# Two tiles of the normed activations in the second feed-forward part: beside the others from the second group on

## What is computed

```python
def conv_gated_mlp(h, w_up, conv_w, conv_b, w_down):
    gate, up = jnp.split(h @ w_up, 2, axis=-1)
    return (jax.nn.gelu(dwconv_centred(gate, conv_w, conv_b), approximate=True) * up) @ w_down
...
    x = x + g2 * conv_gated_mlp(modulate(rmsnorm(x, norm2_g[l]), sh2, sc2), *ffn)
...
    return rmsnorm(x, final_norm_g)
```

## Time and profile before

| | |
|---|---|
| median of 3 runs | 2564.16 us (2562.82 to 2564.85) |
| profiled execution | 2563.17 us, its span 2561.4 us |
| TensorE busy | 2536.9 us, 20794 matmuls |
| VectorE busy | 1927.4 us |
| ScalarE busy | 1138.3 us |
| granted clock of TensorE | 0.997 over the span |
| second feed-forward part | from 1825.5 us on |

### The profile page before, as it was taken

One profiled execution on the slowest core, in us unless ns is written; L12 is line 12 of the kernel. 1 busy time (PEld: TensorE's weight loads), 2 busy tenths in 40 slices (PEclk: granted clock), 3 DMA queues, 4 the chain that ended last, 5 costly groups with the idle time before them and its releaser, 6 DMA issues.

```text
span 2561.4 us, 49562 instructions
## 1 busy us (share of the span) xinstructions
PE 2536.9 (99%) x20794; PEld 2463.2 (96%) x20794; DVE 1927.4 (75%) x2458; ACT 1138.3 (44%) x1223; POOL 0.2 (0%) x4
## 2 busy tenths in 40 slices
PE   9999999999999999999999999999999999999998
PEld 9889999999999999999999899959999999999998
DVE  8978887897999888888893236777766666666667
ACT  6556554444544444444433234433444444444443
POOL 0000000000000000000000000000000000000000
PEclk9999999999999999999999999999999999999999
DMA  8766667767888888888773344424555555556553
GB/s 320 263 231 219 240 231 247 251 239 246 291 285 292 281 286 287 282 289 285 268 260 100 99 165 148 149 73 165 165 198 191 190 197 197 189 191 197 195 188 112
DMA packets 282890, 557.20 MB, mean 218 GB/s; under 512 B 10552, under 2 KB 16985, under 8 KB 282585
## 3 DMA queue, kind: packets, MB, share of 16 engines
q1 hardware_dynamic: 282568, 552.57, 64.3%
q10 hardware_dynamic: 144, 2.10, 0.2%
HBM read 552.53 MB, written 2.10 MB: 217 GB/s over the span
## 4 chain that ended last, share of the span: by engine, by line
PE 92%; DVE 6%; issue 1%; DMA 1%; ACT 0%; SPq 0%; DVEq 0%
PE PS L1826 80%; PE PS L1837 3%; PE PS L1840 3%; PE PS L1839 3%; DVE WL L1003 1%; PE PS L2073 1%; DVE ada1c L1269 0%; DMA RAW<-in_w_in 0%; DVE adac L1427 0%; PE PS L1904 0%; DVE SQ L1029 0%; PE PS L2176 0%; PE PS L2083 0%; PE PS L1893 0%; PE PS L2063 0%
## 5 line engine op out<-in xcount | busy, mean ns | idle before, releaser
L527 ACT ACTIVATE WH<-RAW 128x1024 fp32r<-128x1024 f32 x840 | 889.3, 1061 | 1278.9 <-PE PS L1826 1147.5
L1003 DVE TENSOR_TENSOR WL<-RAW,WH 128x1024 fp32r<-128x1024 f32 x840 | 1017.8, 1222 | 578.4 <-ACT WH L527 569.5
L1826 PE MATMUL PS<-XL,WH 128*128 128x256 f32 x4288 | 664.2, 277 | 0.0
L1826 PE MATMUL PS<-XH,WH 128*128 128x256 f32 x3752 | 586.0, 278 | 1.1 <-ACT WH L527 1.1
L1826 PEld LDWEIGHTS PS<-XL,WH 128*128 128x128 f32 x4288 | 569.1, 188 | 0.0
L1826 PE MATMUL PS<-XH,WL 128*128 128x256 f32 x3752 | 503.2, 277 | 0.0
L1826 PEld LDWEIGHTS PS<-XH,WH 128*128 128x128 f32 x3752 | 498.3, 188 | 3.5 <-DVE XL L1059 1.5
L1826 PEld LDWEIGHTS PS<-XH,WL 128*128 128x128 f32 x3752 | 461.5, 188 | 0.0
L1826 PE MATMUL PS<-HH,WH 128*128 128x256 f32 x1728 | 268.0, 277 | 1.2 <-DVE X L1388 1.2
L1826 PE MATMUL PS<-HL,WH 128*128 128x256 f32 x1728 | 266.2, 276 | 0.0
L1826 PE MATMUL PS<-HH,WL 128*128 128x256 f32 x1728 | 231.1, 276 | 0.0
(11 more groups left out here) (285 smaller groups left out, 1823.0 us busy)
## 6 DMA issues: line engine op xcount, KB each, us to landing
RAW<-in_w_ff SPq DMA_DIRECT2D x128, 1024.0 KB, 5.9
RAW<-in_w_in SPq DMA_DIRECT2D x111, 1024.0 KB, 5.1
RAW<-in_w_up SPq DMA_DIRECT2D x88, 1024.0 KB, 5.0
adab<-in_ada_w SPq DMA_DIRECT2D x128, 512.0 KB, 5.3
RAW<-in_w_down SPq DMA_DIRECT2D x44, 1024.0 KB, 5.0
ada1b<-in_ada_w SPq DMA_DIRECT2D x64, 512.0 KB, 6.0
RAW<-in_w_out SPq DMA_DIRECT2D x32, 1024.0 KB, 5.2
RAW<-in_w_oa SPq DMA_DIRECT2D x8, 1024.0 KB, 5.5
```

Of the source, the lines that this page charges most:

```text
L527: A(WH[:, c.base % 2, hs], RAW[:, c.base % SLOTS, hs], ACT.Copy).then_inc(hi_done, 1)
L1003: tt(WL[:, b, hs], RAW[:, c.base % SLOTS, hs], WH[:, b, hs].bitcast(f32), ALU.subtract)\
L1826: ins = MM(out[:, f, :], w[:, b, kk, f * P:(f + 1) * P], x, start=first and not low and n == 0 and f % 2 == 0, stop=last and low, skip_gro ...
```

## The change

A new buffer, `BEGIN_FIRST`, holds tiles 0 and 1 for the first group of the second feed-forward part alone. It lies at offset AR + 16 K + 96, which is 32 bytes past a multiple of 64, as XH_FIRST is. When ScalarE has written the last quarter of XH it writes tiles 0 and 1 a second time from the same NT and the same shift, now to their place in XH, and counts `first_again`. TensorE waits for that count ahead of the second group, and from then on reads all 16 tiles from XH. All stages before keep XH_FIRST. XL is not changed.

```diff
+        XH_FF2, XH_FF2_BEGIN = XH[:, :, :], XH[:, :, :]
...
+        BEGIN_FIRST = at("BEGIN_FIRST", [P, 2, T], AR + 16 * K + 96, f32r)
...
         def tile_of(x, k):
 
+            if k < 2 and x is XH_FF2_BEGIN:
+                return BEGIN_FIRST[:, k, :]
             return XH_FIRST[:, k, :] if k < 2 and x is XH else x[:, k, :]
...
                             for k in (2 * h, 2 * h + 1):
-                                ins = A(tile_of(XH, k), NT[:, k, :], ACT.Identity, bias=shift(k))
+                                ins = A(tile_of(XH_FF2_BEGIN if norm == N_FF2 else XH, k), NT[:, k, :],
+                                        ACT.Identity, bias=shift(k))
...
                 quarter_high(3)
+                if norm == N_FF2:
+                    for k in range(2):
+                        ins = A(XH_FF2[:, k, :], NT[:, k, :], ACT.Identity, bias=shift(k))
+                    ins.then_inc(sm["first_again"], 1)
...
+                        hi = XH_FF2_BEGIN if norm == N_FF2 else XH
                         for k in (2 * h, 2 * h + 1):
-                            ins = stt(tile_of(XL, k), NT[:, k, :], shift(k), tile_of(XH, k).bitcast(f32),
+                            ins = stt(tile_of(XL, k), NT[:, k, :], shift(k), tile_of(hi, k).bitcast(f32),
                                       ALU.add, ALU.subtract)
...
                 for s in range(SLOTS):
-                    wide(c.plus(s), q, s)
+                    wide(c.plus(s), q, s, xh=XH_FF2)
                 for s in range(SLOTS):
-                    wide(c.plus(4 + s), q.plus(1), s)
+                    wide(c.plus(4 + s), q.plus(1), s, xh=XH_FF2)
...
             for s in range(SLOTS):
-                wide(Place(C_FF2 + s), Place(Q_FF2), s, e=E_NORM4)
+                wide(Place(C_FF2 + s), Place(Q_FF2), s, e=E_NORM4, xh=XH_FF2_BEGIN)
+            pe.wait_ge(sm["first_again"], 1)
             for s in range(SLOTS):
-                wide(Place(C_FF2 + 4 + s), Place(Q_FF2 + 1), s)
+                wide(Place(C_FF2 + 4 + s), Place(Q_FF2 + 1), s, xh=XH_FF2)
```

More of the change, by code:

```diff
@@ L340, in build_program @@
             "pn_done tp_done pt_done pv2_done a2_done fu_ps fu_done fy_ps fq_done fy_ends fy_done mlp_ps mlp_arg mlp_sin hf_ps "
-            "hf_done fold_done ks_ps ks_done zt_ps zt_done zf_ps ys_done yi_ps hz_done mix_sq cw_done conv_a conv_b "
+            "hf_done fold_done ks_ps ks_done zt_ps zt_done zf_ps ys_done yi_ps hz_done mix_sq first_again cw_done conv_a conv_b "
             "conv_done gelu_done").split()
```

## The result

| us | before | after |
|---|---|---|
| median of 20 runs each | 2563.69 (2560.04 to 2566.32) | 2562.06 (2559.23 to 2591.92) |
| the 11 shorter runs of after | | median 2561.11 (2559.23 to 2562.60) |
| the 9 longer runs of after | | median 2588.84 (2584.81 to 2591.92) |
| profiled execution | 2563.17, span 2561.4 | 2588.84, span 2587.0 |

The ratio of the times, after to before, is **1.0038 (1.0020 to 1.0056)**. That is a mean over two kinds of runs: the changed kernel never took 2573 us, it took some 2561 us or some 2589. Its median of 2562.06 says little: had two of the runs gone the other way, it would be over 20 us higher. Eleven runs are 2.6 us faster than before, nine are 25.2 us slower than before. No run of before was longer than 2566.53 us, of 122 in all sessions.

What follows compares the result with a forecast made beforehand. TensorE, busy 2536.9 of 2561.4 us, was taken as the bound. 21 x 0.115 = 2.4 us off the 2564.16 us median, other terms zero, gave 2561.8 us; range: 2561.8 less some 2.8 us to 2564.2 plus 2.3 us.

Steps and rivals of the forecast that it cites:

- The gain: On TensorE, 21 gate and up groups no longer open with XH_FIRST, saving 0.115 us each, 2.4 us in all.
- The place as the cause: XH_FIRST's start 32 bytes past a multiple of 64 makes its group 0.11 to 0.12 us slower on TensorE.
- rival one: The tile's place is not what costs, so the change gains nothing: 2564.2 us; chance 0.09.
- ScalarE's two activations and the wait at no cost: Two activations (0.91 us) have over 6 us of cover; first_again is satisfied 7.3 us before the second group: zero cost.
- The slow pace and its price: A lasting TensorE pace, 117.7 against 113.3 ns, over 6144 matmuls of the remaining 128 chunks: 27.0 us lost.
- rival two: The wait for XL leaves TensorE slow and no XH_FIRST head ends it: 2588.8 us; chance 0.15.
- the word "reset": In before, 236 matmuls from 390.18 us were slow, 164 from 421.24 fast; the XH_FIRST head between seemed to reset the pace.
- the term for a lasting slow pace: TensorE's wait for XL at 1837.06 us should end fast as before, so 0 us was added to the sum.
- Nothing there sets the state off: Between 1850 and 2545 us only stretches with XH_FIRST are slow, so nothing there starts the slow pace.

Runs made afterwards that it cites:

- after_again: The changed kernel run again with nothing edited: 11 runs from 2559.58 to 2563.08 us, none long, ratio 0.9994.
- e_places: e_second with gate groups of steps 0 to 5 reading copies of tiles 0 and 1 at 0, 16, 32, 48, 8, 56 bytes past a multiple of 64: 2567.27 us.
- e_kicks_gate: e_second with 4 + j transposes between gate and up group of each step j, and displaced tiles at every step's gate group: 2578.46 us.
- e_thirteen: The changed kernel with 13 instead of 12 idle products ahead of the first group: 11 runs, 3 long (2587.51 to 2589.07 us), ratio 1.0014.
- e_second: The changed kernel with the second group also reading displaced tiles 0 and 1: medians 2561.13 and 2560.37 us in two sessions, 0 of 22 runs long.
- after_third: The changed kernel with nothing edited, on another chip: 12 runs, 9 from 2560.74 to 2563.00 us, 3 long (2586.16 to 2588.87), ratio 1.0012.
- e_swap: The changed kernel with VectorE making XL's third quarter ahead of NT's last: 12 runs, 5 long (2587.49 to 2591.66 us), ratio 1.0039.
- e_middle: The changed kernel with step 4's gate group reading displaced tiles: 12 runs, 9 from 2559.53 to 2563.29 us, others 2570.78, 2588.67, 2589.20; ratio 1.0014.
- e_middle_up: The changed kernel with step 4's up group reading displaced tiles: 11 runs, median 2561.43 us, none long, ratio 0.9993.
- e_kicks: e_second with 4 + j unread transposes at the start of each step j (0 to 9): 2579.11 us.
- e_eight_head: e_eight with step 4's up group opening with displaced tiles: 10 runs, median 2562.52 us, ratio 0.9997.
- e_eight: e_second with one break of 8 transposes at the start of step 4: 10 runs, median 2561.29 us, none long, ratio 0.9991.

## Why the prediction was partly right and missed

**The gain.** Its term was 21 x 0.115 = 2.4 us. In after_again, whose profile is one of 2561.80 us, the part from the first head to the last chunk is 2.37 us shorter than in before; the medians of the first session differ by 2.6 us (2563.69 to 2561.11). The price, the count and the claim that it all falls off TensorE were right, for an execution that stays fast.

**The place as the cause** (rival one the other way round). Right: e_places has no extra time at offset 0, and 0.08 and 0.15 us at 16 and 32.

**ScalarE's two activations and the wait at no cost.** Right: 0.90 us for the pair, ended at 1841.17, while TensorE came at 1849.22 without idle time.

**The slow pace and its price** (rival two). That the pace is a state that outlasts its cause, and its size, were right: 6144 x 4.4 = 27.0 us. The medians of the two kinds of runs of after are 27.7 us apart, and the profiles of after and after_again differ by 744.63 - 717.09 = 27.5 us; the rest is mostly the 92 or so matmuls between the gap and the second group, 0.4 us. The rival's 2588.8 us is the 2588.84 of the longer kind. The signs it was to be known by are all there: 0.47 us for four matmuls, 22.6 us for a group, 281 ns on HH.

**One reading under that rival was wrong.** The 236 matmuls from 390.18 to 417.96 us are not all on well-placed tiles, and the group that opens at 417.96 us is not the next one. A group opened with XH_FIRST at 395.36 us, was met slow and left TensorE slow (rows under e_kicks_gate). The heads near 56 and 463 us did the same. So the row on which the word "reset" rested held a head that reset nothing.

**The step that failed** is the term for a lasting slow pace, which the sum put at nothing, with the sentence that carried it: "the change puts nothing ahead of 1837.06 that moves a time, so the same wait should end the same way". The runs showed 27.7 us more in 9 of 20 runs, from a slow pace that in the profile starts at that wait, before either new activation and the wait for first_again. The chance of 0.15 went with the sentence. Two things were wrong with it.
- The outcome doesn't follow from the times that were compared at the wait. The gap in six profiles: how TensorE came to it, when it went on, how far that was after the eight matmuls ahead of it were over, and how it left:

| kernel | came | restart, us | late by, us | left |
|---|---|---|---|---|
| before | slow | 1837.06 | 0.09 | fast |
| after_again | slow | 1838.05 | 0.08 | fast |
| e_thirteen | slow | 1837.11 | 0.10 | **slow** |
| e_second | fast | 1838.39 | 0.30 | fast |
| after | fast | 1837.81 | 0.29 | **slow** |
| after_third | fast | 1835.15 | 0.30 | **slow** |

  (The lateness is the restart less the start of those eight and 8 x 117.7 or 113.3 ns.) In the other ten profiles that have the gap (all but e_swap) TensorE came fast, went on 0.30 or 0.31 us late and left fast. So of 13 that came fast two left slow, and of 3 that came slow one did: the same gap to 0.01 us, and either pace behind it. One execution of before was one throw, and I had read it as a rule. That the earlier trace rows show a wait that ended slow was in my hands, and I gave it the weight of an exception.
- The gap isn't the only place. TensorE already came to it slow in 3 of the 16 profiles, and e_swap, without the gap, had 5 long runs of 12. In before neither seems to matter, since 21 heads come after it: none of its 122 runs was long, while 18 of the 77 runs with this gap and without a head in the second group were long (after, after_again, after_third, e_middle, e_middle_up, e_thirteen; the run of 2570.78 us is counted). That a head in before ends a pace still slow at 1848 us is an inference; its one profile left the gap fast.

The consequence is the miss: the measured ratio, 1.0038 (1.0020 to 1.0056), lies on the side to which I had given 0.15, though the median lay in my range. I had also formed a range for one value, while the changed kernel has two. "Nothing there sets the state off" was right for the stretch from 1850 us on, but it was the wrong comfort: nothing there ends it either. The prediction's own sign of being wrong, a slow stretch that starts between 1837 and 2545 us from something else than these tiles, is what the profile shows.

**What stays open.** What decides a throw: the transposes' number weighs (8 of 10 breaks of 8 or 10 went slow, 2 of 32 others) but doesn't decide alone (e_kicks and e_eight_head slow at 8, e_eight fast), and at the gap no time that was compared tells the cases apart. Why the share differs between sessions (9 of 20, 0 of 11, 3 of 12) isn't explained. And why a displaced head at offset 32 ended the slow pace in 7 of 7 cases where a profile shows it in this part (the six above and e_eight_head), but never at the three earlier places, and by the times not in two of the three long runs of e_middle, isn't either. That e_second is free of long runs rests on 0 of 22 runs. Only the first 11 of them tell something: in that session e_middle and e_thirteen had 6 such runs of 23 against 0 of 11, which chance alone would give in about one case of 13.

**The better version** is e_second. One head more, at a price of 0.12 us, keeps nearly all of the gain (2.3 and 2.6 us at the median in two sessions) and showed none of the long runs, though no profile shows its head meeting the slow pace.

## What to carry to other kernels

Before removing something that looks like a small fixed cost on TensorE, ask what it ends: lay the start-to-start distance of equal matmuls along the whole stretch, and look for a pace that lasts beyond its cause. If one profile shows such a pace both starting and stopping at waits, treat each wait as a throw, give the bad outcome a chance near its share of the waits seen, and keep a cheap reset behind the last throw of a long stretch, after looking in a trace whether it really ends the pace at that place. And look at the list of run times, not at the median alone: a kernel with two kinds of runs has a median that tells of neither.

## What the runs showed of the hardware

- TensorE's stream of weight loads and 128x256 matmuls has two lasting paces at the granted clock of 1.00: 113.3 and 117.7 ns. The slow one lasted over 6,200 matmuls in after (1838.39 to 2571 us), while after_again ran the same program fast. The Trainium skill, "TensorE: Matmul & The Clock Gate", section "Wait — 56ns, not 53.3ns?", gives columns / 2.4 GHz and some 2.5 ns for matmuls back to back, which would be 109.2 ns for 256 columns, as an estimate from that page; neither pace of this trace agrees with it.
- The pace was seen to change at a wait of 0.1 to 0.3 us, at breaks of 4, 8, 9 and 10 transposes between matmuls, and at heads whose moving tile starts 32, 48 or 56 bytes past a multiple of 64. Within this part, behind the start of its first group, nothing else was seen to change it.
- The same kind of head, at the same offset of 32 bytes, ended the slow pace at some places and not at others: near 418 and 485 us in 17 of 17 profiles, near 56, 395 and 463 us in none of 17.
- Such a tile's own price, for 24 matmuls of which 16 read it, was 0.08 us at 16 bytes and 0.15 at 32 in e_places (0.12 for XH_FIRST, also at 32).
